# Sliding attention values in a float32 kernel of split products: both halves of V as one stationary tile

## The reference, cut to what matters

```
scores = einsum(q, k) * 64 ** -0.5            # with ALiBi, a mask and a sink
probs  = softmax(concat(scores, sink))[..., :-1]
out    = einsum('bnhgqk,bnkhd->bnqhgd', probs, vv)
ya     = out * silu(gate)
```

## Time and profile before

| | |
|---|---|
| runs | 2794.62, 2789.79, 2789.72 us, median 2789.79 |
| profiled execution | 2790.87 us device time, span 2789.1 us, 33326 instructions |
| TensorE busy | 2732.7 us (98% of the span) |
| VectorE, ScalarE, GpSimd busy | 45%, 36%, 39% |
| mean granted TensorE clock | 0.994 of 2.4 GHz |
| sliding stages | about 161 to 375 us and 860 to 1075 us of the span |

### The profile page before, as it was taken

How to read it: one execution, slowest core, us unless ns; L and a number is a source line. 1 busy time by engine, 2 the same in 40 slices (tenths; PEclk the granted TensorE clock), 3 DMA queues, 4 the chain that set the end, 5 groups by cost and what they waited for, 6 DMA issues and landing times.

```text
span 2789.1 us, 33326 instructions
## 1 busy us (share of the span) xinstructions
PE 2732.7 (98%) x13100; PEld 2271.2 (81%) x13100; DVE 1241.8 (45%) x1831; ACT 1000.0 (36%) x1566; POOL 1089.6 (39%) x544
## 2 busy tenths in 40 slices
PE   8999998999999999899999999999999999999997
PEld 7888887888888888788878888888878888888886
DVE  6466636622346663672335545553443222222223
ACT  5244435523223443553433333332223323332222
POOL 1443332344443433334443333334344444444442
PEclk9999999999999999999999999999999999999998
DMA  6432231254443223124442232222223333336333
GB/s 183 132 84 76 73 121 45 66 142 143 123 132 91 69 76 121 45 67 138 138 120 76 76 83 76 73 80 80 87 83 121 113 109 111 114 113 211 117 125 113
DMA packets 307611, 289.13 MB, mean 104 GB/s; under 512 B 33152, under 2 KB 256000, under 8 KB 306944
## 3 DMA queue, kind: packets, MB, share of 16 engines
q1 hardware_dynamic: 300512, 264.40, 32.0%
q10 hardware_dynamic: 6944, 22.61, 2.1%
HBM read 260.19 MB, written 26.74 MB: 103 GB/s over the span
## 4 chain that ended last, share of the span: by engine, by line
PE 84%; DVE 11%; DMA 2%; ACT 1%; issue 1%; POOL 0%; SPq 0%; DVEq 0%; ACTq 0%
PE bank L873 25%; PE bank L875 24%; PE bank L874 24%; PE work L1131 1%; DMA w_raw<-in_w_in 1%; DVE pt L1728 1%; PE o_bank L874 1%; PE o_bank L875 1%; DVE mixed L1475 1%; PE work L987 1%; PE work L989 1%; PE o_bank L873 1%; DMA latent_scr<-mixed 1%; DVE probs L1680 1%; DVE mixed L1471 1%
## 5 line engine op out<-in xcount | busy, mean ns | idle before, releaser
L850 POOL TENSOR_TENSOR w_lo<-w_raw,w_hi 128x1024 fp32r<-128x1024 f32 (+3 forms) x460 | 982.0, 2137 | 1367.5 <-ACT w_hi L699 1367.5
L873 PE MATMUL bank<-act_in,w_hi 128*128 128x512 f32 x2662 | 1054.0, 396 | 12.8 <-DVE act_in L1443 9.9
L875 PE MATMUL bank<-act_in,w_lo 128*128 128x512 f32 x2662 | 1041.0, 391 | 0.0
L874 PE MATMUL bank<-act_in,w_hi 128*128 128x512 f32 x2662 | 1039.7, 391 | 0.0
L699 ACT ACTIVATE w_hi<-w_raw 128x1024 fp32r<-128x1024 f32 (+3 forms) x468 | 438.0, 937 | 1049.3 <-PE bank L875 648.4
L873 PEld LDWEIGHTS bank<-act_in,w_hi 128*128 128x128 f32 x2662 | 501.0, 188 | 116.8 <-DVE act_in L1443 11.2
L875 PEld LDWEIGHTS bank<-act_in,w_lo 128*128 128x128 f32 x2662 | 500.5, 188 | 107.2
L874 PEld LDWEIGHTS bank<-act_in,w_hi 128*128 128x128 f32 x2662 | 501.2, 188 | 98.9 <-issue 1.7
L873 PE MATMUL bank<-mixed,w_hi 128*128 128x512 f32 x768 | 299.7, 390 | 0.0
L875 PE MATMUL bank<-mixed,w_lo 128*128 128x512 f32 x768 | 299.1, 389 | 0.0
L874 PE MATMUL bank<-mixed,w_hi 128*128 128x512 f32 x768 | 299.0, 389 | 0.0
(11 more groups left out here) (267 smaller groups left out, 2703.7 us busy)
## 6 DMA issues: line engine op xcount, KB each, us to landing
w_raw<-in_w_in SPq DMA_DIRECT2D x512, 128.0 KB, 2.5
w_raw<-in_w_in SPq DMA_DIRECT2D x224, 256.0 KB, 2.9
w_raw<-in_w_out SPq DMA_DIRECT2D x64, 512.0 KB, 3.7
w_raw<-in_w_in SPq DMA_DIRECT2D x32, 512.0 KB, 3.7
w_raw<-in_w_out SPq DMA_DIRECT2D x64, 256.0 KB, 4.6
x_scr<-buf ACTq DMA_DIRECT2D x32, 256.0 KB, 3.2
probs<-x_scr SPq DMA_DIRECT2D x32, 256.0 KB, 5.0
w_raw<-in_w_attn_up SPq DMA_DIRECT2D x32, 256.0 KB, 2.9
```

The source lines that it names most:

```text
L850: nc.gpsimd.tensor_tensor(lo, raw, hi, ALU.subtract).then_inc(lo_ready, 1)
L873: pe.matmul(dst, lhs[0], rhs[0], start=start, stop=False, skip_group_check=skip)
L874: pe.matmul(dst, lhs[0], rhs[1], start=False, stop=False, skip_group_check=skip)
L875: return pe.matmul(dst, lhs[1], rhs[0], start=False, stop=stop, skip_group_check=skip)
```

## The change

The tile `v_swa` loses its zero columns. For each token block and each key/value head it holds the 64 high and the 64 low columns side by side, 128 in all. A block now takes two products. The first has all 128 columns as the stationary operand and the high part of the probabilities moving: partitions 0 to 63 of `o_bank` get high by high, partitions 64 to 127 get low by high. The second has only the 64 high columns as stationary operand and the low part of the probabilities moving, and adds to partitions 0 to 63. The two halves of `o_bank` have to be added. ScalarE copies partitions 64 to 127 into `swa_lo`, and VectorE adds that to partitions 0 to 63 and writes the head's own rows of `swa_sum`. This is done after every head. After head 1 of a pair, VectorE multiplies `swa_sum` with the gate and splits it as before. `o_bank` is now in use by one head at a time, so TensorE waits for `y_done` ahead of every head's values.

```diff
-        ys += 0 if h["kind"] == "swa" and h["e"] == 0 else 1
+        ys += 1
...
-        v_swa = y_flat[:, 0:1536].rearrange("p (s b c) -> p s b c", s=2, b=NB)
+        v_swa = y_flat[:, 0:1024].rearrange("p (b e s c) -> p b e s c", b=NB, e=2, s=2)
+        swa_lo, swa_sum = sq, acc2
...
+        def o_lo_before(h):
+
+            return 16 * h["l"] + 2 * h["h"] + h["e"]
...
+        o_lo = sem("o_lo")
...
@@ ScalarE
+                elif name == "values" and heads[step[1]]["kind"] == "swa":
+                    act.wait_ge(pv_done, step[1] + 1)
+                    act.activation(swa_lo[0:64, :], o_bank[64:128, :], ACT.Copy).then_inc(o_lo, 1)
...
@@ TensorE
-                    if h["y0"] and h["e"] == 0:
+                    if h["y0"]:
                         pe.wait_ge(y_done, h["y0"])
...
                         if kind == "swa":
-                            v = v_swa[:, :, j, 64 * h["e"]:64 * h["e"] + 128]
+                            both = v_swa[:, j, h["e"], :, :].rearrange("p s c -> p (s c)")
+                            pe.matmul(o_bank[:, j * P:j * P + w], both, pt[:, 0, at:at + w],
+                                      start=j == 0, stop=j == NB - 1, skip_group_check=True)
+                            ins = pe.matmul(o_bank[0:64, j * P:j * P + w], both[:, 0:64], pt[:, 1, at:at + w],
+                                            start=False, stop=j == NB - 1, skip_group_check=True)
+                            continue
...
@@ VectorE, swa_values
-                    link(v.memset(v_swa[:, :, :, 64:128].bitcast(F32), 0.0))
                     src = work[1][:, :].rearrange("p (b a c) -> p b a c", b=NB, a=2)
-                    dst = v_swa.rearrange("p s b (a c) -> p s b a c", a=3)
-                    for e in range(2):
-                        link(v.tensor_copy(dst[:, 0, :, 2 * e, :], src[:, :, e, :]))
-                        link(v.tensor_tensor(dst[:, 1, :, 2 * e, :], src[:, :, e, :],
-                                             dst[:, 0, :, 2 * e, :].bitcast(F32), ALU.subtract))
+                    link(v.tensor_copy(v_swa[:, :, :, 0, :], src))
+                    link(v.tensor_tensor(v_swa[:, :, :, 1, :], src, v_swa[:, :, :, 0, :].bitcast(F32), ALU.subtract))
...
@@ VectorE, values
-                    if kind == "swa" and h["e"] == 0:
+                    if kind == "swa":
+                        v.wait_ge(o_lo, o_lo_before(h) + 1)
+                        own = head_rows(h["e"])
+                        ins = v.tensor_tensor(swa_sum[own, :], o_bank[0:64, :], swa_lo[0:64, :], ALU.add)
+                        if h["e"] == 1:
+                            link(ins)
+                            link(v.tensor_tensor(swa_sum[:, :], swa_sum[:, :], gate[:, t % 2, :], ALU.mult))
+                            link(split(y, swa_sum[:, :]))
+                            signal(y_done)
+                        else:
+                            ins.then_inc(y_done, 1)
                         continue
```

More of the change, by code:

```diff
@@ L1164, in _ @@
                                     (pt[:, 0, at:at + w], pt[:, 1, at:at + w]),
-                                    j == 0 and h["e"] == 0 and kind != "sb", j == NB - 1, skip=True)
+                                    j == 0 and kind != "sb", j == NB - 1, skip=True)
                     ins.then_inc(pv_done, 1)
@@ L1736, in _ @@
                     kind, t = h["kind"], h["h"]
-                    if kind == "swa" and h["e"] == 0:
+                    y = mixed[:, 8 + t if kind == "mla" else t]
+                    if kind == "swa":
[9 more added lines that the diff above has]
+                            ins.then_inc(y_done, 1)
                         continue
                     v.wait_ge(pv_done, h["j"] + 1)
-                    y = mixed[:, 8 + t if kind == "mla" else t]
                     if kind == "mla":
@@ L1744, in _ @@
                         continue
-                    link(v.tensor_tensor(tmp[:, 0, :], o_bank[:, :], gate[:, t % 2 if kind == "swa" else 0, :],
-                                         ALU.mult))
+                    link(v.tensor_tensor(tmp[:, 0, :], o_bank[:, :], gate[:, 0, :], ALU.mult))
                     link(split(y, tmp[:, 0, :]))
```

## The result

The changed kernel takes 2864.31 us in the median of 4 runs (2862.29 to 2865.34), against 2789.76 for the kernel before. The ratio is 1.0262, with a 95% interval of 1.0244 to 1.0280: 2.6% slower. Forecast were 2842 us and a range up to 2862. The direction and the place were right, the size was 22 us short, and the median lies 2.3 us outside the range. The profiled execution has a span of 2860.5 us, 71.4 more than before.

What follows compares the result with a forecast made beforehand. The prediction took TensorE, 84% of the chain, as the bound, with VectorE counting where it makes TensorE wait. Terms 39 + 6 - 1 + 8 = +52 us on 2790.87 gave 2842 us, range 2805 to 2862.

Steps and rivals of the forecast that it cites:

- TensorE's part: Value products in the sliding stages: 0.90 us a head instead of 1.37, saving 0.47 us, 15.0 us over 32 heads.
- The drain at a change of shape: Rival, chance 0.05: the 64-column product drains TensorE, eight gaps of 0.16 us in 32 heads, about 2875 us.
- Place of the output in the queues: Copy and add stand ahead of the next head's norm; with GpSimd, second to fourth heads stall 1.0, 4.4, 0.9 us.
- bare stalls: Rival, chance 0.22: VectorE gets large steps in between GpSimd's, no stall long enough to lower the clock; 2804 us.
- The eight groups: Second to fourth heads' stalls less TensorE's saving: +4.9 us per group, +39 us for eight (9 and 50).
- The clock: Half clock behind the third head's stall costs 2 us, taken for half of the eight: +8 us (0 to 16).
- Fourth head's output: Output ahead of the evacuation lengthens the chain: 6 x 0.7, plus 2 x 0.9 at layer ends, together +6 us.
- The values tile: Two 0.7 us operations replace memset and four half-size ones, once a layer, ahead of the first head: -1 us (0 to -1.5).

Runs made afterwards that it cites:

- add_behind_norm: Changed kernel with copy and add one slot behind the next head's norm, first pair's multiply and split behind the fourth head's scores: 2787.37 us, ratio 0.9985.
- three_products: Best version (output taken apart, last split behind the next group's first norm) with twelve 128-column products a head again: 2785.11 us, ratio 0.9973 against the kernel before.
- short_low_parts: Changed kernel with GpSimd computing low parts of the sliding and first gate groups' weights for only 16 columns of a chunk: 2797.89 us, ratio 1.0026.
- copy_on_vector: Changed kernel with VectorE instead of ScalarE copying the lower half, so VectorE no longer waits for ScalarE: 2804.39 us, ratio 1.0046.
- before_split_later: Kernel before the change with only each pair's split moved later, its product going to another tile: 2790.59 us, ratio 0.9995.

## Why the prediction was right and wrong

- **TensorE's part: right.** 0.55 us a head by the changed kernel's rows, 0.56 by the intervals of `add_behind_norm`, 0.46 by `three_products`, forecast 0.47. The drain at a change of shape, a rival with 0.05, is refuted: the spacing is 0.12 us. The Trainium skill, "TensorEngine Tiling (Array Packing)", Key Properties, says that a change of tiling mode drains TensorE. No such gap is in the rows, and they decide. Whether a stationary operand of 64 columns counts there as another mode, no run shows.
- **Place of the output in the queues: right, and at the third head with some luck.** In the first two groups of each layer the stalls are where they were forecast and nearly as long: 0.82, 4.55 and 0.80 us against 1.0, 4.4 and 0.9. The order of the operations at the third head was another. The forecast had the split done ahead of GpSimd's pair, light steps that pass and a large step that waits. In the trace GpSimd came 0.06 us ahead of the split's subtract (184.62 against 184.68). The subtract waited 1.06 us and the four-column addition 0.83, and the large step ran clear in 0.96. Both orders delay the norm by 1.9 us. The rival "bare stalls" was wrong about the kernel itself. `short_low_parts` shows what it would have been: 1.99 us at the third head where I had 2.5, none at the others. `copy_on_vector` shows that place and not amount makes it.
- **The eight groups: right in four, too small in four.** From the first to the fourth transposes of a group the eight groups took 305.6 us before (38.2 each) and 370.9 after, +65.3. Of this 18.3 is the clock. The other 47.0 stand against +39 (bounds 9 and 50). The first two groups of each layer come to 5.1 us each, forecast 4.9. The third have 6.3 and the fourth 7.1, from the waits of 1.88 to 2.00 us behind GpSimd's 128x1024 operations. The forecast took the first group's pair of 1.3 us for all eight.
- **The clock: here the prediction failed.** The step read "I take it for half of the eight, +8 (0 to 16)". Behind all eight stalls the clock halved, and it cost 1.4 to 2.8 us each, 2.3 in the mean: 18.3 us, above the upper bound. The price of 2 came from a window of 4 us that I had chosen in the profile before. In the changed kernel TensorE worked at the half clock from 189.21 to about 195, longer than that window. The rule of the Trainium skill named beside it, "TensorE: Matmul & The Clock Gate", Part 1, pointed the right way, to all eight, and with its 16 the sum was still short. The missing 10 us of this term are the largest part of the 22 us by which the forecast was short; the groups' missing 8 come next.
- **Fourth head's output: right in kind, smaller in the groups.** Six times +0.2 us instead of +0.7, since ScalarE had split the next chunk during the stall and was free earlier. At the end of the first layer's stage it is +0.89 us up to the 4 us wait in `short_low_parts`, where the clock stayed full (64.89 against 64.00), forecast +0.9. In the changed kernel the two layers have 66.44 and 66.85 instead of 64.00 and 65.30. The last head waits 1.99 us there and the clock falls behind it: 10.30 us from its transposes to the wait for a bank, against 8.71. That is 1.6 us twice, for which the forecast had no term.

```profile
1137.00:1141.00 4.00, 4.00 (x13) 3.18 (x12) 1.15 (x2) 0.98 (x2) 1.42 (x1) 0.57 0.61 190
```

- **The values tile: right.** The first transposes come 1.67 us earlier (forecast 1), at 159.11. Of that 0.6 may be scatter, since `before_split_later`, which has the old tile, starts them at 160.15.
- **Not forecast:** behind the 4 us wait of the second layer the trace is another 3 us longer (1657.3 against 1654.3 us from its end to the end of the span). The waits there are nearly the same, the clock is not. Before, it is below 1.00 in 1134 to 1139 (0.66) and then full to 1500. After, it has 0.51 in 1202 to 1209 and 0.57 in 1502 to 1506:

```profile
1202.00:1209.00 7.00, 5.84 (x21) 5.26 (x21) 1.94 (x4) 2.23 (x4) 1.27 (x1) 0.51 0.09 21
1502.00:1506.00 4.00, 4.00 (x18) 3.29 (x18) 2.25 (x11) 2.68 (x3) 1.11 (x1) 0.57 0.37 107
```

By these windows about 3 us more are lost to the half clock, an estimate. Why it differs there is open: it is one trace each.

## What to carry to other kernels

When work is added to an in-order queue, its place counts before its amount: ask what stands behind it and who waits for that, and put ahead only what frees a shared buffer. Removing a stall moves the question to the next entry of the same queue, so look at the new kernel's waits before calling it solved; here it took three versions, from 2864 over 2805 and 2787 to 2776 us. A TensorE wait of several microseconds is to be priced with the slow clock behind it, over the whole stretch at half rate. And rows of one group don't stand for all groups: here the helper engine's operations were larger in the later ones.

## What the hardware did that was not expected

- A wait's length doesn't settle whether the clock falls. All eight stalls of 4.3 to 4.6 us in the changed kernel were followed by the half clock. Of eight equal stalls of 1.99 us in `short_low_parts` two were, and each cost 1.6 us more than the others (intervals of 13.8 against 12.2 us). Nor is the price the same: the stalls of the changed kernel cost 1.4 to 2.8 us.
- Even small VectorE operations wait for GpSimd: an addition of four columns took 0.99 us instead of 0.16 at 186.58, and a scaling of 128 columns took 2.46 instead of 0.29 at 332.40.
- A product with 64 stationary columns started 0.12 us behind one with 128 and the next one 0.11 to 0.12 us behind it, as products of one shape did before. For 128 moving columns the two take 0.12 us together, where three full ones had taken 0.29.
